# Second-table weights on diagonals of 4 tokens in place of 8, and a twelfth row for the second table's ring

## The chip, the cores and the metric

The kernel runs on one core of one Trainium2 chip. Times are device microseconds from start to end of one execution. The engines are TensorE (PE in the profile; its weight loads stand apart as PEld), VectorE (DVE), ScalarE (ACT), GpSimd (POOL) and SyncE (SP). Each works through its own list of instructions in order and waits on semaphores for the others.

## The reference, cut to what matters

The program is one step of a hybrid encoder layer in float32: a mixer (RWKV-7 and differential attention), layer norms, and then PEER, a layer that fetches its weights row by row from two tables of 16,384 rows with 1,024 numbers each. For each token, 8 heads choose 16 rows each, so 128 rows of each table:

```python
idx = jnp.take_along_axis(cidx, sel, axis=-1)          # 128 rows per token
gate = jax.nn.softmax(top, axis=-1)
u = jnp.take(u_tab, idx, axis=0)                       # first table
act = gelu(einsum('thed,td->the', u, xb))
vv = jnp.take(v_tab, idx, axis=0)                      # second table
return einsum('the,thed->td', gate * act, vv)
```

There are 1,024 prompt tokens and 64 sample tokens, that is 8 tiles of 128 tokens and one of 64. A row of a table is 4 KB, so the two fetches of a tile of 128 tokens move 2 x 64 MB, and all tiles some 1.1 GB.

## The kernel before, in words

**Two kinds of work side by side.** The mixer and the choice of rows ("mix steps") run on PE, DVE, ACT and SP, in five segments (four of 256 prompt tokens, one of 64 sample tokens). The table work of the tiles before is laid between the mix steps. Round g holds the first-table work of tile g and the second-table work of tile g-1. `plan()` writes one common order of mix steps and table pieces, and every engine walks through that order. In rounds 1 to 7 pieces lie between mix steps (`spread`); in rounds 8 and 9 no mix step is left and pieces follow each other (`alternate`).

**First table ("u").** A piece is four slots. POOL issues one indirect DMA per slot, which brings one row for each of 128 tokens (128 x 4 KB = 512 KB) into a row of `ring_u`, 8 rows. DVE multiplies it with the tile's tokens and sums (L1460), and then adds one to `u_used`. POOL reuses a ring row when `u_used` says that DVE is through with it.

**Second table ("v").** Here a gather belongs to one token: it brings the 128 rows that this token chose, again 512 KB, into a row of `ring_v`, 11 rows. A piece is four tokens, one from each group of 32 (a "quad") of the tile. PE multiplies the 128 weights of the token with the 128 rows (L1110). It first does the left halves (512 columns) of the four tokens, which wait for the landings, and then the four right halves, each of which adds one to `v_summed`. Gather number n goes to ring row n % 11 and so waits until token n - 11 is summed:

```python
for k in range(PIECE):                                            # v_piece, POOL
    place, times, before = homes[(pieces_before(g) + q) * PIECE + k]
    if before is not None:
        pool.wait_ge(S["v_summed"], before + 1)
```

`ring_homes` gives these numbers. From the 21st piece of tile 7 on (gather number 976), when no first-table work is left to issue, the rows of `ring_u` join as further rows of the second table's ring: 11 + 8 = 19 rows, and the count starts again at row 0.

**The weights of a token.** PE must add a token's result to the row of that token alone. So the weights stand in a matrix of 128 x 32 in which only the token's own column is not zero. `spread_w` holds such matrices for `EIGHTH` = 8 tokens of each quad, on a diagonal, and twice, as two blocks in turn. A tile of 128 tokens has 32 pieces; 8 of them use one block, so there are 4 blocks in a tile (`fills`). ACT fills them. `spread_block(g, b)` waits until PE has summed all tokens of block b - 2, clears the old diagonal (L817), fills the new one (L819) and adds one to `spread_ready`; PE waits for that at a block's first piece. Blocks 0 and 1 of a tile are filled when its round opens. ACT fills a later block k + 1 at the place in the common order at which block k begins on PE:

```python
k, left = divmod(q, block_pieces(g))                              # v_part, ACT
if c == 0 and left == 0 and 1 <= k < fills(g) - 1:
    spread_block(g, k + 1)
```

**Opening of a round.** DVE waits for the last `u_used` and `v_summed`, makes the new weights, PE turns them, ACT copies them out (L836) and fills two blocks, and PE starts on the new tile's tokens.

Of the kernel before, what the change touches and what calls it, by code (L numbers as in the profile page):

```python
# [53 lines left out]
NT = SEG // P  # L54
PIECE = 4
U_ROWS = 8
V_ROWS = 11
BESIDE = 20
QUAD = 32
EIGHTH = 8  # L60

MU, W0, A0, KKW, KAW, RKW, LXG, LXB, SHIFT, SUBG, LNG, LNB = 0, 14, 18, 22, 26, 30, 34, 38, 42, 56, 57, 65
NPAR = 73
# [100 lines left out]
def u_before(g):  # L164
    return sum(u_pieces(x) for x in range(g))
# [13 lines left out]
def pieces_before(g):  # L179
    return sum(v_pieces(x) for x in range(g))  # L180


def fills(g):

    return QUAD // EIGHTH

# [71 lines left out]
def ring_homes():  # L258

    wide_from = (pieces_before(len(TILES) - 2) + BESIDE) * PIECE  # L260
    all_u = u_before(len(TILES)) * PIECE
    times = [0] * V_ROWS + [len(range(row, all_u, U_ROWS)) for row in range(U_ROWS)]
    last, homes = [None] * (V_ROWS + U_ROWS), []
    for n in range(pieces_before(len(TILES)) * PIECE):
        place = n % V_ROWS if n < wide_from else (n - wide_from) % (V_ROWS + U_ROWS)
        times[place] += 1
# [55 lines left out]
def build(nc, ins, outs):  # L322
# [3 lines left out]
    with ctx:  # L326
        def sb(name, shape, dt=F32):
            return ctx.enter_context(nc.sbuf_tensor(name, shape, dt))

        def sem(name):  # L330
            return ctx.enter_context(nc.semaphore(name))
# [54 lines left out]
        ring_u = sb("ring_u", [P, U_ROWS, D])  # L386
        ring_v = sb("ring_v", [P, V_ROWS, D])
        h1 = sb("h1", [P, 4, D])
        dots = sb("dots", [P, SLOTS])
        wgt = sb("wgt", [P, SLOTS])  # L390
        wgt_t = sb("wgt_t", [P, P])
        spread_w = sb("spread_w", [P, 2, P // QUAD, EIGHTH, QUAD])
        st2 = sb("st2", [P, 2, 6])
# [129 lines left out]
        s_u = [sem(f"u_row{r}") for r in range(U_ROWS)]  # L523
        s_v = [sem(f"v_row{r}") for r in range(V_ROWS)]

# [23 lines left out]
        def v_row(place):  # L549

            return (ring_v[:, place, :], s_v[place]) if place < V_ROWS else (ring_u[:, place - V_ROWS, :], s_u[place - V_ROWS])

# [249 lines left out]
        def _(act):  # L802
# [7 lines left out]
            def spread_block(g, b):  # L810

                n, quads = sum(fills(x) for x in range(g)) + b, TILES[g][0].rows // QUAD
                if n >= 2:
                    act.wait_ge(S["v_summed"], (pieces_before(g) + (b - 1) * block_pieces(g if b > 0 else g - 1)) * PIECE)
                    gone = n - 2 - sum(fills(x) for x in range(g - 1)) if b < 2 else b - 2
                    old = TILES[g - 1][0].rows // QUAD if b < 2 else quads
                    tl.link(act.activation(diagonal(n % 2, old, gone), zeros[:, 0:old * EIGHTH].rearrange("p (a b) -> p a b", b=EIGHTH), ACT.Copy))  # L817
                src = wgt_t[:, 0:quads * QUAD].rearrange("p (a b) -> p a b", b=QUAD)[:, :, b * EIGHTH:(b + 1) * EIGHTH]
                act.activation(diagonal(n % 2, quads, b), src, ACT.Copy).then_inc(S["spread_ready"], 1)  # L819

            def diagonal(half, quads, b):

                block = spread_w[:, half, 0:quads, :, :].rearrange("p a t m -> p a (t m)")
                return block[:, :, b * EIGHTH:b * EIGHTH + (EIGHTH - 1) * (QUAD + 1) + 1:QUAD + 1]

# [236 lines left out]
        def _(pe):  # L1062
# [33 lines left out]
            def v_part(g, q, c):  # L1096
# [6 lines left out]
                for k in range(PIECE):  # L1103
                    home, times, before = homes[n * PIECE + k]
                    row, landing = v_row(home)
                    if c == 0:
                        pe.wait_ge(landing, 16 * times)
                    quad, place = v_token(g, q, k)
                    out = slice(quad * QUAD, (quad + 1) * QUAD)
                    x = pe.matmul(pacc[out, c, :], spread_w[:, blocks % 2, quad, place % EIGHTH, :], row[:, c * 512:(c + 1) * 512],  # L1110
                                  start=(place == 0), stop=(place == QUAD - 1), skip_group_check=True)
# [686 lines left out]
```

## Time and profile before

| | us |
|---|---|
| median of 3 executions | 4246.4 (4245.26 to 4247.04) |
| span of the profiled execution | 4199.6 |
| median less span | 46.8 |

The profiled execution has no whole time of its own beside its span; 46.8 us is what lies around the span if that execution is taken to be like the median one. A busy share is an average over stages that differ: the first 710 us hold no second-table gather, and from 4020 us on no first-table gather is left. The chain that the profile follows back from the end reaches to 3003 us.

### The profile page before, as it was taken

What the parts mean: (1) busy time and instruction counts of PE and PEld (TensorE: products, weight loads), DVE (VectorE), ACT (ScalarE), POOL (GpSimd) and SP (SyncE); (2) the same over time, 40 slices, a digit from 0 to 9 for tenths busy, and PEclk for the clock granted to TensorE, in tenths of its full rate; (3) what the DMA queues carried; (4) which work ended last, traced back from release to release, by engine and by line L of the source; (5) the groups of instructions that cost most, each with busy time, mean ns of one, the idle gap of its engine ahead of it and who ended that gap; (6) DMA issues with size and microseconds to landing.
All of it is one profiled execution on the core that took longest, in us unless ns stands there. A gap on an engine that the chain in (4) does not pass through costs nothing. (4 is left out here: it accounts for less than half of the span.)

```text
span 4199.6 us, 48966 instructions
## 1 busy us (share of the span) xinstructions
PE 2858.0 (68%) x18591; PEld 1580.0 (38%) x18591; DVE 2419.6 (58%) x5633; ACT 671.8 (16%) x1913; POOL 2387.5 (57%) x2194
## 2 busy tenths in 40 slices
PE   7887376787746777768567777667545666675566
PEld 5666354445413343446134343344112222330011
DVE  3427977565864555667855555569745465673311
ACT  3331122220011122101012222101011111000000
POOL 0001366665455665675765665665666776676764
PEclk9988677888977787879788987789767767687788
DMA  3125688889788988899998897998999999999997
GB/s 110 69 67 208 226 303 312 313 332 385 288 324 317 347 289 315 331 374 351 352 371 304 336 339 285 338 374 313 373 378 356 360 383 359 388 373 349 370 365 297
DMA packets 371523, 1325.36 MB, mean 316 GB/s; under 512 B 40188, under 2 KB 75416, under 8 KB 360152
## 3 DMA queue, kind: packets, MB, share of 16 engines
q0 software_dynamic: 314576, 1145.45, 72.7%
q1 hardware_dynamic: 56712, 176.79, 11.2%
q8 instruction: 147, 2.41, 0.2%
q14 instruction: 88, 0.72, 0.0%
HBM read 1310.53 MB, written 11.29 MB: 315 GB/s over the span
## 5 line engine op out<-in xcount | busy, mean ns | idle before, releaser
L752 POOL DMA_INDIRECT ring_u<-in_peer_u,idx x1088 | 1222.6, 1124 | 1088.3 <-DVE gates L1703 396.0
L1460 DVE CUSTOM_DVE_ANT_0 ring_u<-ring_u,h 128x1024 f32<-128x1024 f32 x1088 | 1294.2, 1224 | 568.3 <-DMA ring_u<-in_peer_u,idx 447.3
L752 POOL DMA_INDIRECT ring_v<-in_peer_v,idx_t x1042 | 1114.2, 1069 | 686.5 <-PE pacc L1110 347.9
L1110 PE MATMUL pacc<-ring_v,spread_w 128*32 128x512 f32 x4168 | 1029.2, 737 | 470.6 <-DMA ring_v<-in_peer_v,idx_t 343.0
L1110 PEld LDWEIGHTS pacc<-ring_v,spread_w 128*32 128x32 f32 x4168 | 170.5, 121 | 1050.5 <-DMA ring_v<-in_peer_v,idx_t 686.3
L1085 PE MATMUL pm<-arena 64*64 64x64 f32 (+1 forms) x6256 | 375.8, 257 | 273.8 <-issue 147.1
L1071 PE MATMUL pm<-hT,wts 128*128 128x256 f32 (+2 forms) x2656 | 544.9, 365 | 25.1 <-issue 14.0
L1071 PEld LDWEIGHTS pm<-hT,wts 128*128 128x128 f32 x2656 | 465.0, 208 | 144.6 <-issue 78.0
L1085 PEld LDWEIGHTS pm<-arena 64*64 64x64 f32 x6256 | 295.5, 157 | 434.7 <-issue 251.2
L1071 PE MATMUL pm<-wts,hT 128*128 128x384 f32 (+1 forms) x576 | 201.3, 504 | 7.5 <-DMA wts<-in_sets 7.4
L1071 PE MATMUL pm<-wts,mixT 128*128 128x128 f32 (+1 forms) x1152 | 148.2, 283 | 13.1 <-DVEq L541 5.1
L1071 PEld LDWEIGHTS pm<-wts,mixT 128*128 128x128 f32 (+1 forms) x1152 | 138.8, 192 | 32.1 <-issue 31.6
L1071 PEld LDWEIGHTS pm<-wts,hT 128*128 128x128 f32 (+1 forms) x576 | 108.5, 191 | 98.6 <-issue 40.3
L1476 DVE SCALAR_TENSOR_TENSOR h<-h,pacc 128x1024 f32<-128x1024 f32 (+1 forms) x9 | 11.0, 1219 | 216.7 <-remote 125.1
L1613 DVE MEMSET pm<- 64x64 f32 (+1 forms) x48 | 6.2, 130 | 207.6 <-PE pm L1302 153.7
L1090 PE MATMUL pm<-arena,block_in 128*128 128x256 f32 (+1 forms) x360 | 109.6, 425 | 17.1 <-ACT arena L932 12.9
L1713 DVE MAX8 arena<-arena 128x8 f32<-128x128 f32 (+3 forms) x216 | 62.1, 288 | 81.3 <-ACT arena L1035 73.6
L1614 DVE TENSOR_REDUCE arena<-pm 128x1 f32<-128x640 f32 (+8 forms) x56 | 52.0, 928 | 65.9 <-PE pm L1302 47.4
L1460 DVE DVE_READ_ACCUMULATOR2_ANT dots<- 128x1 f32 x1088 | 88.9, 82 | 0.0
L1316 PE MATMUL pm<-arena 128*128 128x128 f32 (+2 forms) x328 | 70.6, 385 | 26.7 <-ACT arena L992 19.9
L1302 PE MATMUL pm<-arena 64*128 64x512 f32 (+4 forms) x224 | 86.8, 570 | 0.1
L1618 DVE RECIPROCAL arena<-arena 128x2 f32<-128x2 f32 (+1 forms) x36 | 5.8, 162 | 132.0 <-ACT arena L981 109.7
(223 smaller groups left out, 2708.2 us busy)
## 6 DMA issues: line engine op xcount, KB each, us to landing
wts<-in_sets SPq DMA_DIRECT2D x82, 1536.0 KB
ring_u<-in_peer_u,idx POOLq DMA_INDIRECT x1088
ring_v<-in_peer_v,idx_t POOLq DMA_INDIRECT x1042
wts<-in_sets SPq DMA_DIRECT2D x11, 1024.0 KB
arena<-in_subkeys SPq DMA_DIRECT2D x5, 1024.0 KB
arena<-in_x_prompt SPq DMA_DIRECT2D x8, 512.0 KB
out<-arena SPq DMA_DIRECT2D x64, 64.0 KB
out<-h POOLq DMA_DIRECT2D x8, 512.0 KB
```

What stands on the lines that cost most here:

```text
L752: pool.indirect_dma_start(out=out, out_offset=None, in_=table, in_offset=bass.IndirectOffsetOnAxis(ap=index.bitcast(U32), axis=0)).then_in ...
L1071: x = pe.matmul(out, lhs(k), rhs(k), start=(k == 0), stop=(k == KT - 1 and not more))
L1085: x = pe.matmul(pm[h, bank, col:col + width], lhs[h], rhs[h], start=start, stop=stop, skip_group_check=True)
L1090: pe.matmul(pm[:, bank, 0:w], ident[:, :], old.rearrange("p c n -> p (c n)")[:, 0:w], start=True, stop=False, skip_group_check=True)
L1110: x = pe.matmul(pacc[out, c, :], spread_w[:, blocks % 2, quad, place % EIGHTH, :], row[:, c * 512:(c + 1) * 512], start=(place == 0), stop ...
L1302: x = pe.matmul(pm[0:r, bank, 0:m], qT[hc, sl(s, t)], keysT[hc, n:n + m], start=True, stop=True)
L1316: x = pe.matmul(pm[0:r, 4, 0:P], attT[0:m, b, 0:r], vals[0:m, b, :], start=(b == 0), stop=(b == nb - 1))
L1460: v.tensor_tensor_reduce(ring_u[:, row, :], ring_u[:, row, :], h1[:, g % 4, :], 1.0, 0.0, ALU.mult, ALU.add, dots[:, slot:slot + 1]).then_ ...
L1476: tl.told(v.scalar_tensor_tensor(x, x, ALPHA, pacc[r, :, :].rearrange("p a n -> p (a n)"), ALU.mult, ALU.add), S["f_read"])
L1613: tl.link(v.memset(sc[0:CH, ..., nk - CH:nk], -1.0e30))
L1614: tl.told(v.tensor_reduce(negm[0:r, of], sc, AX.X, ALU.max, negate=True), S["max_ready"])
L1713: tl.link(v.max(values[:, 0:8], x))
```

## The change

Two constants change.

```diff
-V_ROWS = 11
+V_ROWS = 12
 BESIDE = 20
 QUAD = 32
-EIGHTH = 8
+EIGHTH = 4
```

`spread_w` has 2 x 4 x `EIGHTH` x 32 numbers per partition, 8 KB before and 4 KB now; a ring row is 4 KB. `fills` gives 8 blocks in place of 4, `block_pieces` 4 pieces in place of 8 (in the sample tile 2 in place of 4). Gather n now waits for token n - 12, and for n from 976 on the joined ring has 20 rows.

On POOL, in its first lap (`ring_v` and `ring_u` are the rings; a row of the list stands for so many DMAs in a row, with the semaphore that they wait for):

```order
 L752 DMA ring_v<-in_peer_v,idx_t 128x1024 x4
 L752 DMA ring_u<-in_peer_u,idx 128x1024 [waits u_used] x4
-L752 DMA ring_v<-in_peer_v,idx_t 128x1024 x3
-L752 DMA ring_v<-in_peer_v,idx_t 128x1024 [waits v_summed]
+L752 DMA ring_v<-in_peer_v,idx_t 128x1024 x4
 L752 DMA ring_u<-in_peer_u,idx 128x1024 [waits u_used] x4
 L752 DMA ring_v<-in_peer_v,idx_t 128x1024 [waits v_summed] x4
```

The fourth gather of the third piece waited for the first token of all; now the third piece goes out whole, and the first gather of the fourth piece is the first to wait.

On POOL, where the rings are joined (tile 7's last pieces and the start of tile 8):

```order
 L752 DMA ring_u<-in_peer_u,idx 128x1024 [waits u_used] x4
-L752 DMA ring_v<-in_peer_v,idx_t 128x1024 [waits v_summed] x11
+L752 DMA ring_v<-in_peer_v,idx_t 128x1024 [waits v_summed] x12
 L752 DMA ring_u<-in_peer_v,idx_t 128x1024 [waits u_used] x8
-L752 DMA ring_v<-in_peer_v,idx_t 128x1024 [waits v_summed] x11
+L752 DMA ring_v<-in_peer_v,idx_t 128x1024 [waits v_summed] x12
 L752 DMA ring_u<-in_peer_v,idx_t 128x1024 [waits v_summed] x8
```

The same gathers go out in the same order; only the row in which each lands has changed, and with it the token for which it waits.

On ACT, in the first round with second-table work, a place without a fill before (L929, L932, L981 and L925 are copies and exponentials of mix steps):

```order
 L929 ACTIVATE arena<-pm 128x256
 L932 ACTIVATE arena<-pm 128x256
+L817 ACTIVATE spread_w<-block_in 128x4x4
+L819 ACTIVATE spread_w<-wgt_t 128x4x4
 L981 ACTIVATE arena<-pm,arena 128x384 x2
 L925 ACTIVATE arena<-pm 128x256
```

and further on in that round a place that had one before (L964, L965 and L909 are mix steps too):

```order
 L964 ACTIVATE arena<-pm 128x256
 L965 ACTIVATE arena<-pm 128x128
-L817 ACTIVATE spread_w<-block_in 128x4x8
-L819 ACTIVATE spread_w<-wgt_t 128x4x8
+L817 ACTIVATE spread_w<-block_in 128x4x4
+L819 ACTIVATE spread_w<-wgt_t 128x4x4
 L909 ACT_TABLE_LOAD
 L909 ACTIVATE arena<-pm 128x256
```

Each clear and fill writes half as much, and between two old places a new pair stands. On PE and DVE no instruction is added, removed or moved.

## Rows read from the trace of the kernel before

**Rows 1.** Page, busy time, share of the span and instructions of each engine.

```profile
PE 2858.0 (68%) x18591; PEld 1580.0 (38%) x18591; DVE 2419.6 (58%) x5633; ACT 671.8 (16%) x1913; POOL 2387.5 (57%) x2194
```

**Rows 2.** Waits of POOL: us in total, times, longest us.

```profile
POOL ring_u L752 <- DVE dots L1460: 380.7, 88, 11.6
POOL ring_v L752 <- PE pacc L1110: 347.9, 91, 18.4
...
POOL ring_v L752 <- remote: 58.4, 32, 4.7
```

**Rows 3.** Waits of all engines, same columns.

```profile
PEld pacc L1110 <- DMA ring_v<-in_peer_v,idx_t: 686.3, 369, 16.5
DVE ring_u L1460 <- DMA ring_u<-in_peer_u,idx: 447.3, 119, 17.4
...
ACT spread_w L817 <- PE pacc L1110: 185.6, 8, 79.9
```

**Rows 4.** Timeline of POOL: start us, us, instruction, idle before and what ended it.

```profile
757.42 1.13 POOL L752 DMA_INDIRECT ring_v<-in_peer_v,idx_t  x1 [0.30 <-issue]
761.99 1.10 POOL L752 DMA_INDIRECT ring_v<-in_peer_v,idx_t  x1 [3.44 <-PE pacc L1110]
...
3101.88 0.94 POOL L752 DMA_INDIRECT ring_v<-in_peer_v,idx_t  x1 [14.76 <-PE pacc L1110]
...
3106.85 0.94 POOL L752 DMA_INDIRECT ring_u<-in_peer_u,idx  x1 [0.30 <-issue]
3108.10 0.94 POOL L752 DMA_INDIRECT ring_v<-in_peer_v,idx_t  x1 [0.31 <-issue]
...
4007.59 0.94 POOL L752 DMA_INDIRECT ring_v<-in_peer_v,idx_t  x1 [3.43 <-remote]
```

**Rows 5.** Chain of waits: start us, us, what.

```profile
3057.23 7.35 DMA ring_v<-in_peer_v,idx_t
...
3100.63 1.12 PE pacc L1110 x8
3101.75 0.13 issue
3101.88 0.94 POOL ring_v L752
```

**Rows 6.** Stretches: us; busy of PE, PEld, DVE, ACT, POOL; clock; DMA share; GB/s.

```profile
1400.00:2100.00 700.00, 512.15 (x3298) 281.43 (x3298) 460.61 (x1094) 109.10 (x292) 446.04 (x401) 0.81 0.90 338
2800.00:3500.00 700.00, 422.75 (x2121) 186.03 (x2121) 426.24 (x1092) 88.42 (x277) 465.55 (x440) 0.76 0.95 366
3500.00:3780.00 280.00, 194.24 (x950) 92.54 (x950) 176.96 (x446) 18.68 (x68) 187.82 (x172) 0.72 0.97 368
1010.00:1022.00 12.00, 7.16 (x32) 3.53 (x32) 11.32 (x17) 3.08 (x7) 0.00 (x0) 0.50 1.01 411
1205.00:1211.00 6.00, 4.57 (x24) 2.30 (x28) 5.10 (x11) 3.25 (x10) 0.00 (x0) 0.50 0.01 3
4030.00:4040.00 10.00, 8.34 (x30) 1.42 (x30) 0.00 (x0) 0.00 (x0) 7.56 (x9) 1.00 1.03 409
```

**Rows 7.** Timeline of ACT, columns as in rows 4.

```profile
1013.94 0.25 ACT L817 ACTIVATE spread_w<-block_in 128x32 f32<-128x32 f32 x1
1014.22 0.26 ACT L819 ACTIVATE spread_w<-wgt_t 128x32 f32<-128x32 f32 x1
...
2852.08 0.26 ACT L817 ACTIVATE spread_w<-block_in 128x32 f32<-128x32 f32 x1 [1.61 <-remote]
...
3975.91 0.26 ACT L817 ACTIVATE spread_w<-block_in 128x32 f32<-128x32 f32 x1 [79.88 <-PE pacc L1110]
```

**Rows 8.** Timeline of POOL, last round.

```profile
4116.24 0.93 POOL L752 DMA_INDIRECT ring_v<-in_peer_v,idx_t  x1 [10.16 <-PE pacc L1110]
```

**Rows 9.** Timeline at the start.

```profile
0.74 1.80 POOL L743 MEMSET spread_w<- 128x2048 f32 x1 [0.29 <-POOLq L1779]
...
6.93 1.42 DVE L1421 BATCH_NORM_STATS2 arena<-arena 128x6 f32<-128x512 f32 x2 [6.93 <-PEq L1066]
```

## The prediction

> **What bounds the kernel now.** I read the busy shares first [rows 1]: no engine is above 68%, so no single engine's work sets the time, and the waits have to be read. POOL's come next [rows 2], since all 2176 gathers go through its one list. It waits 380.7 us for first-table rows to come free and 347.9 + 58.4 us for second-table rows ("remote" is a release that the profile can't name). On the other side the consumers wait for what POOL has sent late: PE's weight loads 686.3 us and DVE 447.3 us [rows 3]. So both sides wait for each other: the rings are short of depth, and the mix steps between pieces come unevenly.
>
> Then the timeline of POOL, for where in a piece it waits. A gather takes 0.94 us and the next starts 0.30 us later, 1.24 us in all [rows 4]. Counted down the timeline, the long waits for `v_summed` stand at the fourth gather of a piece and hardly anywhere else: 69 of them over 0.8 us, the first at 762.0, the last at 4007.6, the largest on the late chain 14.76 us at 3101.9 [rows 4]. Without the usual 0.30 us they come to 343 us. The reason is arithmetic: with 11 rows, gathers 4p to 4p+2 wait for tokens of piece p-3, but gather 4p+3 waits for token 4p-8, the first of piece p-2. Tokens are summed only in a piece's right halves, so this last gather waits a whole piece longer than the three before it.
>
> Last the chain of waits. At 3100.63 PE sums tokens, at 3101.88 POOL sends the held gather and the chain stays on POOL [rows 5]; at 3057.23 it goes through the landing of such a gather itself. Nine of the late fourth-gather waits are on it from 3003 us to the last at 4007.6. So POOL's wait does decide, though not everywhere.
>
> **The change part by part: the ring row.** With 12 rows all four gathers of a piece wait for piece p-3. Gather 4p+3 goes at once, then the first-table gathers that stand behind it, and only gather 4p+4 waits, for the very token (4p-8) for which 4p+3 waited before. The release isn't earlier; POOL does more before it. Per wait POOL gains the smaller of the wait and 1.24 us times what it can send ahead: the one gather, and those first-table gathers between it and 4p+4 whose rows are free. At 3101.9 that is 1 + 4 gathers, 6.2 us: gather 4p+4 left at 3108.10 [rows 4] and could leave at 3101.9. Counted so over the 69 waits:
> - 38 waits vanish, 112 us;
> - 9 are cut by 6.2 us each, 56 us;
> - 5 by 3.7 us, where `ring_u` is full after two more, 18 us;
> - 17 by 1.24 us, as the next piece follows directly or `ring_u` is full at once, 20 us.
>
> Sum 207 us of POOL's time, and this is not yet time of the kernel. How much reaches the end? From 3003 us on I can read it off the chain: the nine waits on it carry a relief of 42 us (4.6 at 3019, 7.2 at 3057, 6.2 three times, 1.2 at 3834, then 3.3, 4.0 and 3.1), of 59 us for all waits there. If each is shortened another chain takes over inside; I take 0.6 of 42, 25 us, a judgement between 1, with no other chain close behind, and 0.3. Before 3003 us, where the profile's chain doesn't reach, the waits have 148 us of relief. There mix steps are dense: in 1400 to 2100 us PE is busy 512 and DVE 461 of 700 us [rows 6], so less passes on. Followed back from wait to release, five such waits, with 16 us, lie on the way; the neighbouring ways hold some more. I take 0.15 of 148, 22 us. Ring row: -47 us. Ends: 0 (all turned into other waits) and 0.7 of 207, -145 us.
>
> **The refills.** 9 tiles get 4 blocks more: 36 clears and 36 fills. A pair takes 0.54 us, from 1013.94 to 1014.48 [rows 7], and a smaller operand hardly shortens it. 28 pairs lie in the seven mixed rounds: 15 us on an engine that is busy 16% [rows 1]. I put a fifth on the path, +3 us; ends 0 and +15. Each clear is also a wait on ACT for PE, with the mix steps queued behind it, and DVE and PE waiting for those. Of 185.6 us of such waits [rows 3] nearly all stand in the last two rounds, where no mix step is behind them (79.88 us at 3975.91); of 14 inside mixed rounds four waited, at most 1.61 us [rows 7], 4.9 us together. 28 more at 0.35 us are 10 us on ACT, +2 us on the path. On the other side PE needs a block four pieces after ACT is told to fill it, where it was eight. Four pieces are 32 matmuls with mix work between, against 0.54 us of filling: nothing.
>
> **The rest.** At the join, gather 976 restarts at row 0. With 11 rows that row was last used 8 tokens back, with 12 rows 4 back (972), so the piece before must have landed and be summed. In this trace four first-table gathers stand between, 5 us, and the wait would be about 1 to 3 us: +1. In the last round the fourth-gather wait of 10.16 us [rows 8] gives 1.24 us back, -1; the following gather then waits for the same token. The first memset (1.80 us) halves, but DVE starts only at 6.93 us [rows 9], on data: 0. Opening a round keeps its chain: 0.
>
> Sum: -47 + 3 + 2 + 1 - 1 = -42 us. Against the profiled span: 4199.6 - 42 = 4157.6; with the 46.8 us around it, **4204 us** (the median 4246.4 less 42).
>
> **Rival one: the transfers swallow it.** POOL's standing still is not the DMA engines' standing still. From 1010 to 1022 us POOL sent nothing and the DMA engines carried 411 GB/s of weight sets and norm tables [rows 6]; a gather sent earlier would only have lain longer in the queue. Against it: from 1205 to 1211 us they carried 3 GB/s [rows 6], and over 1400 to 2100 us 338, where 409 is reached at 4030. If only gaps like the second count, and these are then filled once more by waits for `ring_u`, some 10 us are left of the 47, less the 5 of the refills: 4241 us.
>
> The Trainium skill (DMA: Bandwidth & Descriptors, "Where 436 GB/s comes from") holds that transfers between HBM and SBUF are bound at about 358 GB/s per core by the HBM side. By that rule the stretches from 2800 to 3780 us, at 366 and 368 GB/s, would be full, and my 25 us there would fall away: about 4229 us. By that rule the trace disagrees: 409 to 411 GB/s were carried [rows 6], so I give it 0.03 of this rival's 0.20.
>
> **Rival two, slower: ACT is held.** Six times in a mixed round, in place of two, ACT stops until PE has finished a piece. PE itself waits there for a landing, 686.3 us over the program and up to 16.5 us at once [rows 3], 2.5 us per piece over 272 pieces. If ACT inherited that at the 28 new places, with ACT-to-DVE steps behind it, the cost is 28 x 2.5 = 70 us and 15 us of instructions, less 47: 38 us slower, 4284 us. It decides from a mean hold of (47 - 15) / 28 = 1.1 us at the new places. For it: new places stand next to different mix steps, and the ring row lets POOL, not PE, run ahead. Against it: the old ones held 0.35 us on average, and most ACT steps wait for PE anyway.
>
> **Rival three: more arrives.** If the early rounds pass on what the late chain passes on, 0.7, the gain is 145 less 5 us: 4106 us. For it: each wait removed also lets DVE, and so the mix, go on. Against it: the 380.7 us of waits for `u_used` [rows 2] stay and take over.
>
> **How the numbers follow.** My forecast 0.60 (its own range 4150 to 4236), transfers 0.20, ACT held 0.10, more arrives 0.10. The range reaches down more than half way to rival three and up past rival one: 4145 to 4246; outside it lie these two 0.10s, ACT held above and more arrives below. A measurement of this kernel can tell about 0.2%, 8.5 us. Faster by more: the forecast but for 0.02, rival three, and 0.07 of the transfers' case: 0.75. Within: 0.02 and 0.13, that is 0.15. Slower: 0.10.
>
> **What would show it.** POOL's wait for PE at `ring_v` falls from 406 us to about 200, and the long ones stand at the first gather of a piece and no more at the fourth. POOL's waits for `u_used` stay or grow. PE's and DVE's waits for landings fall together by some 50 to 100 us. GB/s in 1400 to 2100 us rises from 338. L817 and L819 have 36 more each, and their waits in mixed rounds stay under 2 us. I am wrong if the fourth-gather waits are gone and the span stands still (rival one), or if ACT's clears there show waits of several us with DVE waiting for ACT after them (rival two).

## The result: slower by 0.9 per cent, and the profile after

The changed kernel takes 4273.45 us (median of 11 executions, 4257.09 to 4310.22), the kernel before in the same set 4246.4 us (11 executions, 4213.9 to 4278.69). The ratio is 1.0088, with a 95% interval of 1.0063 to 1.0113: between the medians that is 27 us longer, where a fall of 42 was forecast; between the means it is 37. The ratios here and below are an estimate of the record that leaves out its slow executions, while the medians are of all, so the quotient of two medians can differ from the ratio by up to 0.3 per cent (here it is 1.0064). The forecast of 4204 us and its range up to 4246 us were both missed, and so was the direction.

The profiled execution took 4262.77 us with a span of 4260.9 us, so only 1.9 us lie around a span. The "46.8 us around it" of the prediction were something else: that profiled execution of the kernel before was itself some 45 us quicker than the median execution, and quicker than any of the 11. Since the forecast was in effect the median less 42 us, this slip did not move it, but differences of 40 us between two single traces of this kernel mean little. The two traces compared below are 61 us apart, more than twice the distance of the medians.

The page after, busy time of each engine, answers to [rows 1]:

```profile
PE 2863.6 (67%) x18591; PEld 1595.9 (37%) x18591; DVE 2418.7 (57%) x5633; ACT 682.0 (16%) x1985; POOL 2409.0 (57%) x2194
```

The work is the same, with 72 more instructions on ACT for 10 us. The waits of all engines (us in total, times, longest), which answer to [rows 2, 3]:

```profile
POOL ring_u L752 <- DVE dots L1460: 639.9, 116, 15.9
PEld pacc L1110 <- DMA ring_v<-in_peer_v,idx_t: 537.6, 322, 13.7
PEld pacc L1110 <- issue: 516.2, 620, 29.6
...
DVE ring_u L1460 <- DMA ring_u<-in_peer_u,idx: 335.5, 101, 15.0
```

```profile
POOL ring_v L752 <- PE pacc L1110: 122.6, 63, 15.5
POOL ring_v L752 <- remote: 48.3, 27, 3.7
```

The ring row did what was said of it. POOL's wait for second-table rows fell from 406 to 171 us. By position in a piece (my count over the timeline) 157 us of it now stand at the first gather and 11 us at the fourth. The late one of [rows 4], gather 675 there, is now gather 676, the first of its piece:

```profile
3166.03 0.93 POOL L752 DMA_INDIRECT ring_v<-in_peer_v,idx_t  x1 [15.49 <-PE pacc L1110]
3167.26 0.93 POOL L752 DMA_INDIRECT ring_v<-in_peer_v,idx_t  x1 [0.30 <-issue]
```

No wait vanished there, but POOL had sent five gathers more before it (it is the 1477th of all, where the other was the 1472nd).

Landings come earlier: PE's and DVE's waits for them fell by 149 and 112 us, 261 us together, far more than the 50 to 100 forecast for both. But POOL's wait for first-table rows rose by 259 us, and the consumers wait for other things: the transfer rate from 1400 to 2100 us, which was to rise, fell. The stretches, with the columns of [rows 6]:

```profile
1400.00:2100.00 700.00, 505.17 (x3254) 283.55 (x3254) 443.53 (x1064) 108.89 (x303) 426.89 (x382) 0.79 0.86 322
2800.00:3500.00 700.00, 408.10 (x2133) 197.73 (x2131) 415.03 (x1054) 82.98 (x269) 452.06 (x423) 0.74 0.92 353
3500.00:3780.00 280.00, 176.15 (x922) 94.18 (x922) 164.65 (x385) 23.13 (x86) 189.96 (x173) 0.70 0.98 381
```

322 GB/s stands where 338 stood, and TensorE's granted clock is 0.79 for 0.81; PE, DVE and POOL do fewer instructions in the first stretch (3254, 1064 and 382 for 3298, 1094 and 401). So the rows arrive earlier and the mix work between them goes slower. Counted by instruction of PE, the lag behind the kernel before is at most 19 us up to 1750 us of the kernel before, 24 at 2050, 41 at 2600, 60 at 3000, 72 at 3487, and 55 at 4127. From the opening of one round (L1476) to the next, rounds 2 to 6 take 4, 15, 16, 17 and 12 us longer, and round 7 is 17 us shorter.

**What the added time is.** PE works in order and has the same work, so the lag can be split by what ended PE's idle time. Between the two traces, 61 us apart, PE's idle time grew by 60 us where the profile names nothing that it waited for ("issue"; 475 us before, 535 now), by 24 us in waits for ACT and by 8 in waits for DVE, and fell by 37 in waits for landings. The two largest parts of it, kernel before, changed kernel, and the kernel with the smaller blocks alone in the quicker setting of the next section (us in total, times, longest):

```profile
PE pacc L1110 <- issue: 132.8, 93, 23.6
PE pm L1085 <- issue: 165.3, 93, 15.1
```

```profile
PE pacc L1110 <- issue: 179.1, 107, 29.2
PE pm L1085 <- issue: 173.2, 103, 22.9
```

```profile
PE pacc L1110 <- issue: 0.8, 3, 0.3
PE pm L1085 <- issue: 2.8, 6, 0.6
```

**How PE comes to stand longer.** One place shows it. At the start of the third segment's mix work PE does two groups of 16 matmuls on L1071, and ACT copies the result of each. The groups wait for nothing in their middle. PE, then ACT, changed kernel (start us, us, instruction, idle before and what ended it; "remote" is a release that the profile can't name):

```profile
1229.84 7.07 PE L1071 MATMUL pm<-hT,wts 128*128 128x256 f32 x32
```

```profile
1231.00 0.20 ACT L858 ACTIVATE arena<-prev 128x1 f32<-128x1 f32 x1
1254.79 0.17 ACT L860 ACTIVATE prev<-pm 128x1 f32<-128x1 f32 x1 [23.58 <-remote]
1254.85 0.38 ACT L861 ACTIVATE arena<-pm 128x256 f32<-128x256 f32 x1
1255.12 0.20 ACT L858 ACTIVATE arena<-prev 128x1 f32<-128x1 f32 x1
1265.39 0.17 ACT L860 ACTIVATE prev<-pm 128x1 f32<-128x1 f32 x1 [10.07 <-remote]
```

By the records the matmuls end at 1236.9. ACT gets the first group's result at 1254.79, the second's at 1265.39, and PE's next matmul starts at 1265.55, 28.6 us after the last. PE itself stands, in work that waits for nothing. The Trainium skill (Perfetto Trace Analysis, "Tensor Engine Instruction (MATMUL, LD_WEIGHTS)") holds that a matmul's end in a profile is worked out from its size and not observed. This trace agrees: a recorded end of 1236.9 stands beside results at 1265.4. Now POOL beside it, in the kernel before and in the changed one:

```profile
1246.93 0.95 POOL L752 DMA_INDIRECT ring_v<-in_peer_v,idx_t  x1 [0.30 <-issue]
1248.18 0.94 POOL L752 DMA_INDIRECT ring_v<-in_peer_v,idx_t  x1 [0.30 <-issue]
1256.09 1.04 POOL L752 DMA_INDIRECT ring_v<-in_peer_v,idx_t  x1 [6.97 <-PE pacc L1110]
```

```profile
1252.21 0.94 POOL L752 DMA_INDIRECT ring_v<-in_peer_v,idx_t  x1 [0.30 <-issue]
1253.46 0.93 POOL L752 DMA_INDIRECT ring_u<-in_peer_u,idx  x1 [0.31 <-issue]
...
1259.81 0.93 POOL L752 DMA_INDIRECT ring_u<-in_peer_u,idx  x1 [0.30 <-issue]
1268.90 1.44 POOL L752 DMA_INDIRECT ring_u<-in_peer_u,idx  x1 [8.15 <-DVE dots L1460]
```

In the kernel before POOL stops at 1249.12, at a fourth gather of a piece, one of the 69 waits that the change removes. PE goes on at 1252.2, 3.1 us later. In the changed kernel POOL sends that gather and six of the first table behind it, stops at 1260.74, and PE goes on at 1265.55. Seven gathers at 1.24 us are 8.7 us; PE's stand grew from 19.1 to 28.6 us, by 9.5. What I counted as POOL's gain is here time in which the transfers go on and PE stands.

But this stand is not by itself time lost at the end. The lag of the changed kernel is 3.8 us ahead of it, 13.3 right behind it and 3.1 again some 20 us later. In the kernel before PE stands a second time there, behind another late result of L1071, at a DMA rate of 410 GB/s (PE, then ACT):

```profile
1279.33 1.22 PE L1170 MATMUL pm<-gate_in,lora_g 128*128 128x256 f32 x2 [10.35 <-ACT arena L861]
```

```profile
1278.83 0.17 ACT L860 ACTIVATE prev<-pm 128x1 f32<-128x1 f32 x1 [13.30 <-remote]
```

The changed kernel goes from its L1071 to L1170 without idle time. One stand of 28.6 us has taken the place of two, 19.1 and 10.4 us.

The same 920 us further on, changed kernel: stretches, then POOL, then ACT.

```profile
2160.00:2186.00 26.00, 0.00 (x0) 0.00 (x0) 9.20 (x16) 0.54 (x3) 16.72 (x18) 0.51 1.03 409
2187.00:2190.00 3.00, 3.00 (x16) 0.67 (x12) 2.62 (x5) 2.94 (x5) 0.00 (x0) 0.50 0.05 15
```

```profile
2180.97 0.94 POOL L752 DMA_INDIRECT ring_u<-in_peer_u,idx  x1 [0.30 <-issue]
2190.04 1.44 POOL L752 DMA_INDIRECT ring_u<-in_peer_u,idx  x1 [8.13 <-DVE dots L1460]
```

```profile
2186.53 0.17 ACT L860 ACTIVATE prev<-pm 128x1 f32<-128x1 f32 x1 [23.33 <-remote]
```

PE does nothing for 26 us at a DMA rate of 409 GB/s. From 2181.9 on POOL waits for DVE, DVE for ACT, ACT for PE; only the transfers run. They run out at 2186 (15 GB/s behind it), and at 2186.5 PE is back. Its granted clock is at the 1.2 GHz level by then (0.51 and 0.50). In the kernel before the stand at this place is 8.4 us and ended while POOL went on sending, at some 409 GB/s; so a stand can also end under full transfers. Here too most of the difference is taken back: the lag is 22 us ahead of the stand, 43 behind it and 25 some 35 us later, after PE in the kernel before has waited 11.0 us for ACT at the same L1170. Rounds 3 and 5, which hold neither of these places nor the like one in round 6, lose as much as round 4.

To size this over a trace, I took each ACT or DVE instruction that waited over 1 us for a semaphore of PE, and the time from the recorded end of the last matmul that raised it to the instruction's start, but no more than the instruction's own idle time. These "late releases", those over 0.6 us, come to 646 us in the kernel before and 750 us in the changed one; those over 3 us to 487 (70 of them, longest 20.0) and 615 us (83, longest 25.2). They lie beside each other in part, so the sums are no time of the kernel. Releases are partly unrecorded in these traces, so a single one may be misread; the groups above are not, since PE's own next matmul is late with them.

### The profile page after: what moved, and what is told of

Same layout as the page of the kernel before. It is cut to its first block, busy times and chain, and to the rows that moved or that the text cites. A ratio compares the mean times of both kernels' runs of the same rounds, so it can differ in the third digit from the quotient of the medians.

```text
span 4260.9 us, 49074 instructions
## 1 busy us (share of the span) xinstructions
PE 2863.6 (67%) x18591; PEld 1595.9 (37%) x18591; DVE 2418.7 (57%) x5633; ACT 682.0 (16%) x1985; POOL 2409.0 (57%) x2194
## 4 chain that ended last, share of the span: by engine, by line
PE 30%; DVE 21%; issue 17%; another core or an unknown queue 10%; POOL 10%; DMA 7%; ACT 4%; DVEq 0%; ACTq 0%; SPq 0%; PEldq 0%
PE pacc L1110 8%; PE pm L1071 7%; PE pm L1085 7%; DVE ring_u L1460 6%; POOL ring_v L752 5%; POOL ring_u L752 5%; DMA ring_v<-in_peer_v,idx_t 4%; DMA ring_u<-in_peer_u,idx 2%; PE pm L1090 2%; DVE arena L1714 2%; PE pm L1302 2%; DVE arena L1715 2%; DVE arena L1717 2%; PE pm L1316 2%
## 5 line engine op out<-in xcount | busy, mean ns | idle before, releaser
L752 POOL DMA_INDIRECT ring_u<-in_peer_u,idx x1088 | 1246.7, 1146 | 1342.9 <-DVE dots L1460 639.9
L1110 PE MATMUL pacc<-ring_v,spread_w 128*32 128x512 f32 x4192 | 1007.3, 734 | 483.0 <-DMA ring_v<-in_peer_v,idx_t 303.7
L1071 PE MATMUL pm<-hT,wts 128*128 128x256 f32 (+2 forms) x2656 | 551.1, 366 | 69.5 <-issue 42.0
L1071 PEld LDWEIGHTS pm<-hT,wts 128*128 128x128 f32 x2656 | 470.2, 210 | 187.8 <-issue 103.0
L1071 PE MATMUL pm<-wts,hT 128*128 128x384 f32 (+1 forms) x576 | 202.4, 507 | 7.0 <-DMA wts<-in_sets 7.0
L1071 PE MATMUL pm<-wts,mixT 128*128 128x128 f32 (+1 forms) x1152 | 150.2, 284 | 10.9 <-DVEq L541 5.2
L1071 PEld LDWEIGHTS pm<-wts,mixT 128*128 128x128 f32 (+1 forms) x1152 | 140.5, 193 | 30.1 <-issue 28.3
L1071 PEld LDWEIGHTS pm<-wts,hT 128*128 128x128 f32 (+1 forms) x576 | 108.7, 191 | 96.6 <-issue 37.8
L1476 DVE SCALAR_TENSOR_TENSOR h<-h,pacc 128x1024 f32<-128x1024 f32 (+1 forms) x9 | 11.0, 1220 | 206.4 <-PE pacc L1110 122.2
```

The source lines that it names most:

```text
L752: pool.indirect_dma_start(out=out, out_offset=None, in_=table, in_offset=bass.IndirectOffsetOnAxis(ap=index.bitcast(U32), axis=0)).then_in ...
L1071: x = pe.matmul(out, lhs(k), rhs(k), start=(k == 0), stop=(k == KT - 1 and not more))
```

## The experiments

The sets of runs fell into two settings, told apart by the kernel before alone: 4196 to 4246 us, mean granted clock some 0.80 (the first result, and the sets labelled r2, r4, r6), and 3826 to 3829 us, clock some 0.85 (e, r3, r5). The expectations speak of chips: on record each set has a chip number, 12, 4 and 3 for r2, r4 and r6, and 5, 10 and 3 for e, r3 and r5 (none for the first result). Number 3 stands in both, so the number alone does not tell the setting. I call them the 4200 setting and the 3800 setting. Kernels are compared only within a set. The letters of the theories are explained in the expectations themselves, anew from the set r3 on.

**Taking the change apart.** Ring row alone, room for it made by leaving out the second norm's shift vector, a part of the computation (its gain is used in its place; the lines that load and use it are cut here):

```
-V_ROWS = 11                       +V_ROWS = 12
-ln2 = sb("ln2", [P, 2, D])        +ln2 = sb("ln2", [P, 1, D])
```

> Ring of 12 rows, diagonals of 8 tokens as before (the second norm's shift vector is left out, its gain is used in its place, to make room for 4 KB). Theory A (the deeper ring is what costs: gathers sent earlier crowd the mix work's transfers or POOL, and the wait only moves to ring_u): slower than before by 0.5 to 1.2%, POOL's wait for u_used near 640 us. Theory B (the refills of ACT cost: 36 more clears and fills in other places): faster than before by 0 to 1%, as I had forecast for the ring row alone (-47 us).

Smaller blocks alone:

```
-EIGHTH = 8                        +EIGHTH = 4
```

> Ring of 11 rows, diagonals of 4 tokens: the refills alone. Theory A: same as before within 0.2%. Theory B: slower than before by 1% or more (the change's 0.9% and what the ring row gains). My prediction had +5 us for this half.

Both parts, each of the second table's first 976 gathers held until the token eleven before it is summed (cut):

```
 place, times, before = homes[number]
+if 11 <= number < 976:
+    before = number - 11
```

> The changed kernel with its 12 rows and diagonals of 4, but a gather waits for token n - 11 as with 11 rows (up to the joined ring). Theory A: the time of before, within 0.3%. Theory B: slower than before, like the changed kernel or more. If the places of the tiles in SBUF matter, it is slow too while e2 is not.

3800 setting (before: 3828.63 us): ring row 3815.77, ratio 0.9963 [0.9947, 0.9979]; blocks 3827.82, 1.0005 [0.9994, 1.0017]; held 3830.91, 1.0010 [0.9998, 1.0022]. The row gains 14 us, the blocks cost nothing, and holding the gathers takes the gain back: the depth does it. But in the first result the change as a whole was slower; so it stands beside its halves once more.

> The changed kernel once more, with its two halves beside it on the same chip. The three kernels of the first comparison ran on a chip on which the kernel before takes 3829 us and not 4246; there the ring row alone brought -0.37% and the refills alone +0.05%. Theory C (the result depends on the chip: where PE is granted less clock and waits are longer, more is sent ahead at the wrong moment): if the kernel before takes about 4246 us here, this one is slower by 0.6 to 1.2%; if about 3829 us, it is faster by 0.2 to 0.4%, the sum of its halves. Theory D (the two halves add up wrongly together, on any chip): slower by 0.5% or more on this chip too, though its halves are not.

> The ring row alone (diagonals of 8; the second norm's shift vector left out). Theory C on a chip of 4246 us: slower by 0.5 to 1.2%, as the ring row is what sends ahead; on a chip of 3829 us -0.3 to -0.5% again. Theory B (the refills are what costs on the slower chip): faster than before by 0.3% or more on either.

> The refills alone (ring of 11 rows). Theory C: within 0.3% of before on either chip. Theory B: slower by 0.9% or more on a chip of 4246 us.

4200 setting (before: 4245.63 us): changed kernel 4281.45, 1.0090 [1.0056, 1.0125]; ring row alone 4295.12, 1.0102 [1.0065, 1.0138]; blocks alone 4254.85, 0.9997 [0.9963, 1.0031]. The same row costs 43 us here and gains 14 there. The blocks, and with them ACT's refills, are out in both.

**Which depth.** Ten rows in place of eleven (`V_ROWS = 10`, blocks of 8), and the 4 KB of the smaller blocks at a ninth row of the first table (`U_ROWS = 9`, `V_ROWS = 11`, `EIGHTH = 4`), beside the changed kernel and the held one.

> The changed kernel once more, as the measure beside which the other three kernels of this set are read, since the twelfth row of the second table's ring stood at ratio 0.996 to 1.001 beside a kernel before of 3828 us and at 1.009 to 1.010 beside one of 4246 us. Theory A (what the row costs belongs to the chip on which the mix work runs slowly and GpSimd waits for the consumers): 1.009 where the kernel before takes 4246 us, 1.000 where it takes 3829 us. Theory B (the cost of the row is a matter of chance between runs of one kernel): a ratio anywhere between 0.997 and 1.012, with an interval that overlaps 1.

> Twelve rows and blocks of 4 tokens, but gather n of the second table waits until row n-11 has been summed, as with eleven rows, so that no gather starts earlier than it could with eleven. Theory A (it is the earlier start of the gathers that costs, that is the depth in use): ratio 1.000, within 0.003, and GpSimd's waits as before: some 380 us on ring_u and 350 to 400 us for the second table's rows, where the changed kernel shows 640 and 125 to 170. Theory C (it is the place of the row in the memory, the twelve separate landing semaphores or the change of which row follows which that costs, and not the depth): ratio 1.009 as the changed kernel, with the waits of before.

> Ten rows for the second table in place of eleven, and nothing else changed from the kernel before (blocks of 8 tokens; 4 KB a partition stay unused). Theory A as a straight line (each row that the second table can run ahead costs about 1 per cent where the mix work is slow): ratio 0.990 to 0.995 on a chip of 4246 us, with GpSimd's wait for the second table up from 348 to some 550 us and the wait on ring_u down from 381 to some 200 us. Theory D (eleven is near the best: fewer rows starve TensorE, more rows take the consumers out of step): ratio 1.005 to 1.015 at ten. On a chip of 3829 us both expect 1.003 to 1.010, since there the landings are waited for.

> The 4 KB that the smaller blocks free go to a ninth row of the first table's ring in place of a twelfth of the second's (nine and eleven rows, blocks of 4 tokens). Theory E (in the changed kernel GpSimd stands at ring_u, 640 us in place of 381, because the second table runs ahead and the eight rows of the first become the limit; a row there relieves exactly the wait that grew): ratio 0.990 to 0.998, the wait on ring_u down to some 200 us and the waits at the second table up. Theory A in its wider form (any row more in flight costs, whichever table it belongs to): ratio 1.005 to 1.015 on a chip of 4246 us. On a chip of 3829 us: 0.995 to 1.000 by both.

3800 setting again (before: 3829.47 us): changed 3812.28, 0.9961 [0.9947, 0.9975]; held 3831.08, 1.0015 [0.9999, 1.0030]; ten rows 3837.52, 1.0029 [1.0015, 1.0043]; ninth row of the first table 3813.17, 0.9960 [0.9942, 0.9977]. Theory B (chance) falls: beside the first result and r2, with 1.0088 and 1.0090, no value between is met. More depth is better here, in either table.

> Twelve rows, blocks of 4, each gather of the second table held until row n-11 has been summed. It stood at 1.001 and 1.0015 beside a kernel before of 3829 us, where the held start takes back all of the 0.4 per cent that the row gains. On a chip of 4246 us, which is wanted here: Theory A (the earlier start costs) 1.000 within 0.003, GpSimd's waits 380 us on ring_u and 350 to 400 at the second table; Theory C (place, semaphores or order of the rows) 1.009. On a chip of 3829 us again 1.001.

> Ten rows in place of eleven, blocks of 8. It stood at 1.0029 on a chip of 3829 us. On a chip of 4246 us: Theory A as a straight line 0.990 to 0.995; Theory D (eleven is near the best) 1.003 to 1.015.

> The 4 KB at a ninth row of the first table's ring, nine and eleven rows, blocks of 4. It stood at 0.996 on a chip of 3829 us, as the twelfth row of the second table did. On a chip of 4246 us: Theory E (a row where GpSimd waits most helps) 0.990 to 0.998; Theory A in its wider form (any row more in flight costs) 1.005 to 1.015.

4200 setting (before: 4196.14 us): held 4204.80, 1.0020 [0.9981, 1.0060]; ten rows 4189.13, 0.9976 [0.9937, 1.0016]; ninth row 4204.14, 1.0014 [0.9984, 1.0044]. The held kernel has the twelve rows, their places and their semaphores; POOL's waits in it are 370 us at `ring_u` and 393 at `ring_v`, as before the change, and its interval ends below the 1.009 of theory C. That speaks for theory A, the earlier start costs. It is a comparison across sets: the changed kernel was not run in this one, whose kernel before is 50 us quicker, and its lowest interval, in r2, begins at 1.0056, just where this one ends (1.0060). The ninth row of the first table neither helps (E) nor costs a per cent (A, wider form); POOL's wait at `ring_u` stayed at 377 us, where E had it fall to some 200. Ten rows may gain a little or nothing; theory A as a straight line had 0.990 to 0.995.

**Whether PE's late releases are the cause.** Theory F says so, theory G calls them a hole in the records. Eight rows (`V_ROWS = 8`, blocks of 8), and a paced supply, from eleven rows and blocks of 4:

```
+pace = sb("pace", [P, 128])
 # ahead of each of the first 976 gathers of either table (cut)
+tl.link(pool.memset(pace[:, :], 0.0))
```

> The changed kernel beside the two others of this set. Theory F (formed from the traces so far: on the chips of 4200 to 4250 us what waits for TensorE is released 3 to 28 us after the recorded end of the matmul that releases it, while the DMA engines move 400 to 415 GB/s without a gap, and in the changed kernel the longest of these end where the transfers run out; a deeper ring lets the transfers run on longer before GpSimd stands, and so lengthens them): on a chip of 4200 to 4250 us ratio 1.009, and the longest such delays 20 to 28 us; on a chip of 3829 us ratio 0.996 and no such delay over 2 us. Theory G (these delays are only a hole in the records and cost nothing): they would be there in equal length with eight rows and with a slower supply.

> Eleven rows and blocks of 4 tokens, and on GpSimd, ahead of each of the first 976 gathers of either table (the rounds with mix work), a memset of 128 columns into a tile that nobody reads and a wait for its end: by the memsets of 256 and 2048 columns of the kernel before (0.31 and 1.80 us) about 0.2 us, with the wait 0.3 us, so that a gather follows its forerunner after some 1.5 us in place of 1.24 and GpSimd by itself supplies no more than some 350 GB/s in place of 423. Theory F: on a chip of 4200 to 4250 us the delays over 3 us behind TensorE fall from 70 to under 25, their longest under 10 us, TensorE's unexplained stalls of 17 to 29 us ahead of tokens 144, 400 and 652 go, and the time is 0.98 to 1.005. Theory G: the delays stay, and the slower supply costs 2 to 4 per cent. On a chip of 3829 us, where the landings are waited for all along, both expect 1.03 to 1.06.

> Eight rows for the second table in place of eleven, blocks of 8, nothing else. Theory F: on a chip of 4200 to 4250 us the longest delays behind TensorE fall to 10 to 14 us (the transfers run out three gathers or some 4 us earlier than with eleven rows), which is worth 20 to 40 us, against which stand more waits for landings: ratio 0.99 to 1.01. Theory G: the delays stay at 17 to 20 us and the time rises 1 to 2 per cent. On a chip of 3829 us both expect 1.01 to 1.02, after 1.003 for ten rows.

3800 setting once more (before: 3826.07 us): changed 3813.41, 0.9966 [0.9951, 0.9982]; paced 4164.39, 1.0888 [1.0861, 1.0916]; eight rows 3883.04, 1.0159 [1.0129, 1.0188]. Nothing is late behind PE in any of them, nor in the profiles of the sets e and r3: 3 or 4 releases over 0.6 us a trace, none over 1.6. The pace is 1.43 us a gather, and costs more than the 3 to 6 per cent expected.

> The paced kernel again (eleven rows, blocks of 4, a memset of 128 columns and a wait for its end ahead of each of the first 976 gathers of either table). Beside a kernel before of 3826 us it stood at 1.089, with 1.43 us from gather to gather (365 GB/s) and no late release behind TensorE, as no kernel has there. On a chip of 4200 to 4250 us: Theory F (TensorE's late releases come of transfers at 400 GB/s and more) expects the sum of delays over 0.6 us, 589 to 787 us in the seven profiles taken there so far, to fall under 250 us, none over 10 us, and since this gives back most of what the slower supply costs, a ratio of 0.98 to 1.02. Theory G (a hole in the records, or a fault of that chip which the transfers have no part in) expects the same sum of delays as ever, and a ratio of 1.03 to 1.06. On a chip of 3829 us again 1.089.

> Eight rows for the second table again, 1.016 beside a kernel before of 3826 us. On a chip of 4200 to 4250 us: Theory F expects the longest delays behind TensorE at 10 to 14 us in place of 17 to 20 and a ratio of 0.99 to 1.005; Theory G 17 to 20 us and 1.01 to 1.02.

4200 setting (before: 4245.92 us): **paced 4219.15, 0.9908 [0.9875, 0.9942]**; eight rows 4273.75, 1.0062 [1.0023, 1.0101]. The pace that costs 8.9 per cent in one setting gains in the other, 0.9 per cent by the ratio, 0.6 by the medians (6 executions beside 16). The place shown above, paced kernel, 4200 setting (its lines are 5 further down: L1076 is L1071): stretch, PE, ACT.

```profile
1218.00:1229.00 11.00, 9.55 (x49) 6.68 (x52) 0.35 (x1) 1.31 (x8) 8.80 (x16) 1.00 0.98 366
```

```profile
1221.59 7.07 PE L1076 MATMUL pm<-hT,wts 128*128 128x256 f32 x32
1228.92 1.50 PE L1115 MATMUL pacc<-ring_v,spread_w 128*32 128x512 f32 x12 [0.26 <-issue]
```

```profile
1225.30 0.17 ACT L865 ACTIVATE prev<-pm 128x1 f32<-128x1 f32 x1 [2.98 <-PE pm L1076]
1228.76 0.17 ACT L865 ACTIVATE prev<-pm 128x1 f32<-128x1 f32 x1 [2.92 <-PE pm L1076]
```

At 366 GB/s the results reach ACT 3.7 and 7.2 us after the start, and PE goes on 0.26 us after its last matmul. And the blocks-alone kernel in the 3800 setting, at 398 and then 410 GB/s:

```profile
1160.54 7.07 PE L1071 MATMUL pm<-hT,wts 128*128 128x256 f32 x32
1167.87 1.06 PE L1110 MATMUL pacc<-ring_v,spread_w 128*32 128x512 f32 x8 [0.26 <-issue]
```

```profile
1160.00:1168.00 8.00, 7.74 (x39) 6.34 (x42) 1.83 (x3) 1.36 (x8) 6.17 (x7) 1.00 1.02 398
1168.00:1180.00 12.00, 1.79 (x16) 0.34 (x11) 11.55 (x21) 1.79 (x4) 8.95 (x11) 0.72 1.02 410
```

No lateness here at the full rate: the rate alone does not make it, the setting and the rate together do. Over the profiles of the 4200 setting (each one execution; stands of PE at three fixed places, after the mix work's first matmuls in rounds 2, 4 and 6; late releases over 3 us; PE's idle time in the whole trace for which the profile names nothing, "unnamed", and its waits for landings, us; ratio):

```
rows of 2nd table     stands, us        sum   over 3 us, sum (count)  unnamed  landings  ratio
8                     10.4  3.9 18.8    33    433 (73)           394       377  1.006
10                    17.2 17.5 20.5    55    426 (67)           459       338  0.998
11, before            19.1  8.4 23.6    51    487 (70)           475       358  1
11, blocks of 4       19.4 19.3 22.9    62    489 (79)           469       339  1.000
12, held              18.5 18.2 23.0    60    498 (79)           478       331  1.002
11, and 9 of 1st      18.8 18.9 20.8    59    483 (73)           517       323  1.001
12, changed           28.6 29.2 24.1    82    615 (83)           535       321  1.009
12, changed again     10.5 27.8 24.9    63    647 (90)           604       311  1.009
12, blocks of 8       27.7 28.7 24.6    81    532 (76)           619       289  1.010
11, paced              0.3  0.3  1.2     2     45  (7)           107       587  0.991
```

The trace with the ninth first-table row is of the longest of its 12 executions. **PE's unnamed idle time** follows the depth in use over the whole program: 394 us with eight rows, 459 to 478 with ten, eleven and twelve held, 517 with the ninth row of the first table, 535 to 619 with twelve in use, 107 with the pace, and 3 to 5 us in every trace of the 3800 setting. The waits for landings go the other way. The change is the balance of the two: +60 and -37 us in its first trace beside the kernel before, +135 and -28 in its second beside the blocks-alone kernel of the same set. That goes with the depth and is not a separate test of it: each number is from one trace.

Theory G falls: with the slower supply the late releases go (201 us over 0.6 us where 589 to 787 stood; one over 6 us, of 19.5 at 4130 us, where the supply is no longer paced), and the time falls though the supply is slower. Theory F was right on the ratio and the sum, but wrong in allowing no delay over 10 us. The first two stands go with the depth: 4 to 10 us with eight rows, 17 to 19 with ten and eleven (8.4 once), and with twelve in use 28 to 29 (10.5 once); held back to eleven they are 18. The third hardly does, 19 to 25. The sums follow the time only roughly: blocks of 8 with twelve rows has 532 us and the same ratio as 615 and 647. At eight rows theory F expected stands of 10 to 14 us and 0.99 to 1.005: the longest was 18.8, and waits for landings outweighed what was saved. Nor did its reason hold for the first two stands, that the transfers run out sooner. All 23 stands of 17 us or more in the table end 2.7 to 4.8 us after POOL's last gather, as the transfers run out; the four short ones without the pace (10.4 and 3.9 with eight rows, 8.4 before, 10.5 in the second trace of the change) ended while POOL sent on at some 410 GB/s.

## Why the prediction was wrong

- **The ring row, -47 us: this step failed**, by sign in the 4200 setting. The row alone measured +43 us there (0.0102 of 4246; interval +28 to +59) and -14 us in the other. Its working was right as far as POOL: the long waits left the fourth gathers, and 235 us of POOL's wait at `ring_v` went, where 207 were counted. What failed is the factor from POOL to the end, 0.6 on the late chain and 0.15 before it. Every saving was taken as worth between nothing and all; I gave the ring row the ends 0 and -145, so no case with a cost was let in. What the runs showed in its place: in the 4200 setting the twelfth row in use brings PE 60 to 150 us more of idle time with nothing named to wait for, against 28 to 50 us less of waits for landings (changed beside before; changed and ring row alone beside blocks alone in r2). POOL's stop also lets the transfers run out, and PE, caught in mix work, mostly came back then.
- Even in the 3800 setting the factor was three times too large: 14 of 207 us reach the end. There the consumers wait more for landings (842 and 640 us in the blocks-alone kernel for 686 and 447 in [rows 3]) and POOL less (266 us for `ring_u` and 136 for `ring_v`, for 381 and 406 in [rows 2]), so the row relieves less.
- **The refills, +3 and +2 us: within the error.** Blocks alone measured 0.9997 and 1.0005. ACT's clears are 70, 36 more; all their idle time (kinds of release, us, times), for 185.6 us in [rows 3]:

```profile
  remote: 230.8, 8
  PE pacc L1110: 144.8, 13
```

  In mixed rounds eight waited, five of them under 3.2 us, two 5.3 and 8.6, and one 55 us at 3672 in a round that was nonetheless 17 us quicker. Waits of several us were the sign that I had set for rival two (ACT is held). It named the right side, but its cause, the blocks, costs nothing when it stands alone.
- **Join, last round, first memset:** not measured apart; too small to tell.
- **Rival one (the transfers swallow it)** had 0.20 and gave 4241: it saw that idle POOL is not idle DMA, but priced a full queue at nothing, where it had a price. Of the signs listed, the GB/s decided: it fell from 338 to 322 with the `v_summed` waits gone, which none of my cases allowed.
- **What the trace before did show and I passed over:** ACT idle for 17.72 us at 1252.19, released by "remote", behind matmuls recorded as done at 1233, and the 19.1 us stand of PE beside it with nothing to wait for. I read "remote" and "issue" as gaps in the records, though the idle PE so marked comes to 475 us there.

What stays open: why PE stands. The profile shows the stand, its company (409 to 411 GB/s) and its end, and no resource. I looked at one candidate, the fetching of PE's instructions, which I take to be the 147 packets of 16 KB on a queue of their own. By the Trainium skill (Runtime: NRT & Kernel Launch, "Instruction fetch mechanics") the sequencer fetches such blocks ahead by DMA, mostly hidden. The trace of the kernel before has them at 1209.27 and 1255.04 us, none while PE stood from 1233.1 to 1252.2, and in the changed kernel none in the three long stands; that speaks against it, but no run tested it. Nor is it shown what makes a setting slow. That the change's 27 us come from PE's unnamed idle time is read off sums of single traces 61 us apart, and no run with twelve rows in use took that idle time away. The three fixed places, 31 us more in one trace of the changed kernel and 12 in the other, are not where it collects, as most of it is made good right behind the first two; which stands are not made good is open. No kernel here is best in both settings: the paced one is best at 4246 us (0.991) and far behind at 3826, the changed one and the ninth first-table row are best at 3829 (0.996). A milder pace, or one with twelve rows, was not tried.

## What to carry to other kernels

A queue's stop can be another engine's relief: before removing a wait of the engine that feeds the DMA engines, look at what the consumers do while the transfers run full, and give the case in which they suffer a price and a chance. An engine that stands in the middle of a group that waits for nothing, or a waiter released many microseconds after the recorded end of its releaser, is a finding and not noise, if it comes back at the same program place in a second trace. Sum such idle time over the program and follow the lag past the place before giving it a price: a long stand can be made good within 20 us. And measure a change of buffer depth in more than one setting: here depth and pace changed sign between two.

## What the runs showed of the hardware

- The same kernel before took 4196 to 4246 us in four sets and 3826 to 3829 us in three, at granted clocks of some 0.80 and 0.85. The first 398 us, without gathers, were equally long in both: the settings part when gathers run beside the mix work.
- In the 4200 setting TensorE stood up to 29 us in or just behind matmuls that waited for nothing, while the DMA engines carried 400 GB/s and more; at the same place with 366 GB/s it did not. In the 3800 setting it did not at 398 to 410 GB/s either. Its idle time with nothing named comes to 394 to 619 us a trace in the one setting (107 with the pace) and to 3 to 5 us in the other.
- A memset of 128 columns and the wait for its end ahead of a gather made 1.43 us of 1.24 us from gather to gather: 8.9 per cent more time in the 3800 setting, 0.6 to 0.9 per cent less in the 4200 setting.
